# Storing the expert results of a mixture-of-experts layer through GpSimd with an index for each half row

## The reference

```python
g_idx = top_k(softmax(t @ rg_w + rg_b), 1)          # one of 4 groups
e_val, e_idx = top_k(softmax(e_logits of group), 2)  # two of its 8 experts
act = silu(t @ w_gate[e]) * (t @ w_up[e])            # 2048 -> 512
out = sum over the token's two experts of comb * (act @ w_down[e])   # 512 -> 2048
x = LN2(alpha * x + gate2 * out)
```

## Time and profile before

| | |
|---|---|
| median of three runs | 1796.48 us (1789.88 to 4247.93) |
| the profiled execution | 1792.82 us, span of the core 1791.0 us |
| TensorE's granted clock, mean | 0.968 |
| DMA, mean over the span | 332 GB/s, 593.75 MB |

### The profile page before, as it was taken

One profiled execution on the slowest core, in us unless ns is written; L12 is line 12 of the kernel. 1 busy time (PEld: TensorE's weight loads), 2 busy tenths in 40 slices (PEclk: granted clock), 3 DMA queues, 4 the chain that ended last, 5 costly groups with the idle time before them and its releaser, 6 DMA issues.

```text
span 1791.0 us, 23326 instructions
## 1 busy us (share of the span) xinstructions
PE 1676.3 (94%) x8973; PEld 723.8 (40%) x8974; DVE 487.6 (27%) x1288; ACT 286.0 (16%) x574; POOL 99.9 (6%) x168
## 2 busy tenths in 40 slices
PE   4999999999998998999999999999999999999994
PEld 2557555473443453333333333333333333333332
DVE  6556435130432554311111111110111111110115
ACT  3110000241223222111111111111111111111111
POOL 5001000410301000100000000000000000000010
PEclk9899999998899996999999999999999999999997
DMA  9996878941679315879989999999999999999963
GB/s 297 385 371 217 312 282 300 273 130 68 230 282 375 130 71 211 352 281 423 422 350 365 423 423 422 423 422 423 422 423 423 422 423 422 423 422 423 422 237 139
DMA packets 125446, 593.75 MB, mean 332 GB/s; under 512 B 13753, under 2 KB 18649, under 8 KB 66473
## 3 DMA queue, kind: packets, MB, share of 16 engines
q1 hardware_dynamic: 105984, 547.95, 76.6%
q0 software_dynamic: 9136, 24.54, 4.3%
q10 hardware_dynamic: 10274, 20.53, 3.2%
HBM read 565.78 MB, written 27.16 MB: 331 GB/s over the span
## 4 chain that ended last, share of the span: by engine, by line
PE 62%; DMA 33%; DVE 3%; ACT 1%; issue 1%; SPq 0%; POOL 0%; DVEq 0%; ACTq 0%; POOLq 0%
DMA ring<-in_exp_w_up 31%; PE bank L690 15%; PE bank L2251 6%; PE bank L707 5%; PE bank L2159 5%; PE bank L2008 4%; PE bank L665 3%; PE bank L333 3%; DMA ring<-in_ada_w 3%; PE bank L2202 2%; PE bank L2091 2%; PE bank L669 2%; PE bank L1986 2%; PE bank L678 1%; PE bank L755 1%; PE bank L1998 1%
## 5 line engine op out<-in xcount | busy, mean ns | idle before, releaser
L690 PE MATMUL bank<-ring,BC 128*64 128x512 f32 x2176 | 496.7, 595 | 32.9 <-DMA ring<-in_exp_w_up 32.0
L690 PEld LDWEIGHTS bank<-ring,BC 128*64 128x64 f32 x2176 | 178.7, 137 | 344.5 <-issue 268.9
L707 PE MATMUL bank<-ring,BC 128*64 128x512 f32 x1088 | 241.0, 595 | 0.0
L562 DVE TENSOR_TENSOR BC<-BC,bank 64x512 f32<-64x512 f32 x34 | 23.5, 692 | 501.0 <-ACT BC L625 501.0
L665 PE MATMUL bank<-H,BC 128*64 128x512 f32 x560 | 150.9, 599 | 1.7 <-DVE H L1871 1.7
L707 PEld LDWEIGHTS bank<-ring,BC 128*64 128x64 f32 x1088 | 75.1, 137 | 140.0 <-issue 135.9
L2251 PE MATMUL bank<-ring,MT 128*128 128x512 f32 x224 | 102.2, 610 | 1.0 <-issue 0.7
L2159 PE MATMUL bank<-ring,MT 128*128 128x512 f32 x192 | 85.4, 598 | 1.0 <-ACT X L1079 1.0
L625 ACT ACTIVATE BC<-bank 64x512 f32<-64x512 f32 x34 | 20.0, 589 | 394.4 <-PE bank L690 394.4
L665 PEld LDWEIGHTS bank<-H,BC 128*64 128x64 f32 x560 | 42.8, 136 | 90.8 <-issue 87.4
L669 PE MATMUL bank<-H,BC 32*64 32x512 f32 x280 | 75.2, 613 | 0.0
(11 more groups left out here) (528 smaller groups left out, 1499.5 us busy)
## 6 DMA issues: line engine op xcount, KB each, us to landing
ring<-in_exp_w_gate SPq DMA_DIRECT2D x128, 1024.0 KB, 21.5
ring<-in_exp_w_up SPq DMA_DIRECT2D x128, 1024.0 KB, 23.5
ring<-in_exp_w_down SPq DMA_DIRECT2D x128, 1024.0 KB, 20.7
ring<-in_ada_w SPq DMA_DIRECT2D x96, 1024.0 KB, 7.4
ring<-in_w_in SPq DMA_DIRECT2D x20, 1024.0 KB, 8.8
y_dram<-BC ACTq DMA_DIRECT2D x68, 256.0 KB, 7.8
ring<-in_w_out SPq DMA_DIRECT2D x16, 1024.0 KB, 10.2
y_dram<-X POOLq DMA_DIRECT2D x4, 1024.0 KB, 11.3
```

Of the source, the lines that this page charges most:

```text
L690: mm = pe.matmul(bank[64 * i:64 * i + 64, 2, :], xT[:, q // 2, k % 4, 64 * (q % 2):64 * (q % 2) + 64], ring[:, j, 512 * (k % 4):512 * (k % ...
L707: mm = pe.matmul(bank[64 * (c % 2):64 * (c % 2) + 64, 4 + c // 2, :], aT[:, j, :], ring[:, 8 + j, 512 * c:512 * c + 512], start=(j == 0), ...
```

## The change

GpSimd gets the same loop over the blocks and issues one indirect DMA for each block. It has 128 indices, one for each partition of YS: an index is a half row (4 KB) of `y_dram`, seen as 5120 half rows of 1024. The index of an empty slot is set beyond the bound, and the DMA has a bounds check that drops it without an error. VectorE works out the indices in each block with three small operations (`rows_of`) and a cast. The columns of a row are thus stored in the order q = 0, 2, 1, 3, and the tail reads them so (`y_cols`, `R_Q`). ScalarE issues no DMA in the loop.

The four early DMAs of zeros go. In their place GpSimd fills all of `y_dram` with 20 DMAs of 1 MB, from the constants in `con`, once the last weights before the experts have landed.

```diff
-    r[:, R_Q] = i // NS + 4 * SLOTS
+    r[:, R_Q] = i // NS % 2 * 2 + i // NS // 2 + 4 * SLOTS
+    r[:, R_W] = NO_ROW + 2 * (i % SLOTS) + i // SLOTS
...
+        def y_cols(q):
+            at = q % 2 * 2 + q // 2
+            return slice(512 * at, 512 * at + 512)
...
         def moe_pool(pool):
+            last = (len(plan) - 1) % PRE_RING
+            pool.wait_ge(landed[last], 16 * last_slot_uses[last])
+            for r in range(0, NBLK * SLOTS, P):
+                pool.dma_start(y_dram[r:r + P, :].rearrange("p (i n) -> p i n", i=4), spread_mid(con[:, 0:512], 4))\
+                    .then_inc(S("y_written"), 16)
...
+            def body(e):
+                pool.wait_ge(S("rint_ready"), since("rint_ready") + 3)
+                pool.wait_ge(S("y_row"), e)
+                pool.indirect_dma_start(y_dram.rearrange("r (c n) -> (r c) n", c=2),
+                                        bass.IndirectOffsetOnAxis(ap=y_row[:, :], axis=0),
+                                        YS[:, :, :].rearrange("p j n -> p (j n)"), None,
+                                        bounds_check=2 * NBLK * SLOTS - 1, oob_is_err=False)\
+                    .then_inc(S("y_written"), 16)
+            pool.wait_ge(S("rint_ready"), since("rint_ready") + 3)
+            expert_loops(pool, body, 1)
             tail_pool(pool)
...
+            def rows_of(e):
+                V.scalar_tensor_tensor(out=edge_past, in0=row_edge, scalar=row_at, in1=edge_sign,
+                                       op0=ALU.is_le, op1=ALU.mult, accum_out=row_valid).then_inc(S("row_valid"), 1)
+                dve.wait_ge(S("row_valid"), e + 1)
+                V.tensor_scalar(row_valid, row_valid, -float(NO_ROW), row_at, ALU.mult, ALU.add).then_inc(S("row_found"), 1)
+                dve.wait_ge(S("row_found"), e + 1)
+                V.tensor_scalar(row_at, row_at, 2.0 * SLOTS, None, ALU.add).then_inc(S("row_next"), 1)
+                dve.wait_ge(S("row_next"), e + 1)
...
                 select(e + 2)
+                dve.wait_ge(S("y_written"), Y_FILLED + 16 * e)
+                rows_of(e)
                 dve.wait_ge(used, len(plan) + (e + 1) * RING)
-                dve.wait_ge(S("y_written"), 32 * e + 32)
                 V.tensor_copy(YS[:, 1, :], bank[:, 5, :]).then_inc(S("ys_dve"), 1)
+                dve.wait_ge(S("ys_dve"), e + 2)
+                dve.wait_ge(S("ys_act"), e + 2)
+                V.tensor_copy(y_row[:, :], row_valid).then_inc(S("y_row"), 1)
...
+               V.tensor_scalar(row_edge[:, 0:E], first_of, 2.0 * SLOTS, float(NO_ROW), ALU.mult, ALU.add),
+               V.tensor_copy(row_at, rc[:, R_W:R_W + 1]),
+               V.memset(edge_sign[:, 0:E], 1.0), V.memset(edge_sign[:, E:], -1.0))
+            go(V.scalar_tensor_tensor(out=row_edge[:, E:], in0=count, scalar=2.0, in1=row_edge[:, 0:E],
+                                      op0=ALU.mult, op1=ALU.add))
...
-                act.wait_ge(S("y_written"), 32 * e + 32)
+                act.wait_ge(S("y_written"), Y_FILLED + 16 * e)
                 nc.scalar.copy(YS[:, 0, :], bank[:, 4, :]).then_inc(S("ys_act"), 1)
-                act.wait_ge(S("ys_act"), e + 2)
-                act.wait_ge(S("ys_dve"), e + 2)
-                for c in range(2):
-                    act.dma_start(y_dram[bass.ds(e * SLOTS, SLOTS), :].rearrange("s (j c n) -> c s j n", j=2, c=2)[c],
-                                  YS[64 * c:64 * c + 64, :, :]).then_inc(S("y_written"), 16)
...
-                for r in range(E * SLOTS, NBLK * SLOTS, P):
-                    n = min(P, NBLK * SLOTS - r)
-                    pool.dma_start(y_dram[r:r + n, :].rearrange("p (i n) -> p i n", i=4), spread_mid(zeros[0:n, :], 4))\
-                        .then_inc(S("spare_out"), 16)
...
-                act.wait_ge(S("spare_out"), 16 * -(-XB * SLOTS // P))
```

More of the change, by code:

```diff
@@ L44 @@
 BIG = 1e30
+NO_ROW = 65536
+Y_FILLED = 16 * NBLK * SLOTS // P
 NROW = 9
@@ L67 @@
 R_T = R_P + 1
-R_LTS = R_T + T // SLOTS + 1
+R_W = R_T + T // SLOTS + 1
+R_LTS = R_W + 1
 R_N = R_LTS + P
@@ L103, in constants @@
     r[:, R_P] = i
-    r[:, R_T:R_LTS] = [0] + [SLOTS * k + 1 for k in range(1, T // SLOTS + 1)]
+    r[:, R_W] = NO_ROW + 2 * (i % SLOTS) + i // SLOTS
+    r[:, R_T:R_W] = [0] + [SLOTS * k + 1 for k in range(1, T // SLOTS + 1)]
     m = np.zeros((P, M_N), np.float32)
@@ L228, in build @@
         slot_i = sb("slot_i", [P, 3, 2], I32)
+        y_row = sb("y_row", [P, 1], I32)
         sink = sb("sink", [P, NH])
@@ L493, in build, with expert_loops @@
         hi = slice(64, 128)
-        def expert_loops(eng, body):
-            with eng.Fori(0, E) as it:
+        row_edge = MODf[:, 1024:1024 + 2 * E]
+        edge_sign, edge_past = MODf[:, 1088:1088 + 2 * E], MODf[:, 1152:1152 + 2 * E]
+        row_at, row_valid = MODf[:, 1216:1217], MODf[:, 1217:1218]
+        def y_cols(q):
+            at = q % 2 * 2 + q // 2
+            return slice(512 * at, 512 * at + 512)
+        def expert_loops(eng, body, start=0):
+            with eng.Fori(start, start + E) as it:
                 body(it)
             extra = eng.value_load(rint[0:1, 0:1], min_val=0, max_val=XB)
-            with eng.Fori(E, NBLK) as it:
-                with eng.If(extra > it - E):
+            with eng.Fori(start + E, start + NBLK) as it:
+                with eng.If(extra > it - (start + E)):
                     body(it)
@@ L529, in moe_sp, with moe_dve @@
             tail_sp(sp)
-        def moe_dve(dve, rows_done, go, end_of, first_of, behind, lg, gm, m1, m2):
+        def moe_dve(dve, rows_done, go, count, end_of, first_of, behind, lg, gm, m1, m2):
             V = nc.vector
@@ L577, in moe_dve @@
                V.tensor_scalar(rsm[:, 6, 1:3, 0:2], slot_f[:, 0:2, :], float(SLOTS), None, ALU.add),
-               V.tensor_scalar(behind[0:1, 0:1], end_of[0:1, E - 1:E], float(E), None, ALU.subtract))
+               V.tensor_scalar(behind[0:1, 0:1], end_of[0:1, E - 1:E], float(E), None, ALU.subtract),
+               V.tensor_scalar(row_edge[:, 0:E], first_of, 2.0 * SLOTS, float(NO_ROW), ALU.mult, ALU.add),
[3 more added lines that the diff above has]
+                                      op0=ALU.mult, op1=ALU.add))
             V.tensor_reduce(xf[0:NBLK, 0:1].unsqueeze(2), after.unsqueeze(1), AX.X, ALU.add).then_inc(S("xf_ready"), 1)
@@ L630, in body @@
                 act.wait_ge(used, len(plan) + (e + 1) * RING)
-                act.wait_ge(S("y_written"), 32 * e + 32)
+                act.wait_ge(S("y_written"), Y_FILLED + 16 * e)
                 nc.scalar.copy(YS[:, 0, :], bank[:, 4, :]).then_inc(S("ys_act"), 1)
-                act.wait_ge(S("ys_act"), e + 2)
-                act.wait_ge(S("ys_dve"), e + 2)
-                for c in range(2):
-                    act.dma_start(y_dram[bass.ds(e * SLOTS, SLOTS), :].rearrange("s (j c n) -> c s j n", j=2, c=2)[c],
-                                  YS[64 * c:64 * c + 64, :, :]).then_inc(S("y_written"), 16)
             act.nop().then_inc(S("ys_act"), 1)
-            act.nop().then_inc(S("y_written"), 32)
             rows_out(0)
@@ L650, in moe_act @@
             extra = expert_loops(act, body)
-            act.wait_ge(S("y_written"), 32 * (extra + E) + 32)
+            act.wait_ge(S("y_written"), 16 * (extra + E) + Y_FILLED)
             act.nop().then_inc(S("y_all"), 1)
@@ L761, in tail_pe @@
                     for i in range(2):
-                        y = Y[:, b, i, 512 * q:512 * q + 512]
+                        y = Y[:, b, i, y_cols(q) if b < 2 else slice(0, 512)]
                         mm = pe.matmul(bank[:, at, :], DW[:, b, i, :], y, start=(i == 0), stop=(i == 1))
@@ L777, in tail_act @@
                     act.wait_ge(S("x_sum"), 2 + 4 * b + q)
-                    nc.scalar.activation(Y[:, b, 1, c], X[:, b, c], ACT.Square, accum_out=S2[:, b, 1, q:q + 1])\
+                    nc.scalar.activation(Y[:, b, 1, y_cols(q)], X[:, b, c], ACT.Square, accum_out=S2[:, b, 1, q:q + 1])\
                       .then_inc(S("x_sq"), 1)
@@ L800, in block @@
                     c = slice(512 * q, 512 * q + 512)
-                    add(Y_FROM[b] + q + 1, Y[:, b, 0, c], Y_BANKS[b][q], G2[:, c], X[:, b, c], S2[:, b, 0, q:q + 1])
+                    add(Y_FROM[b] + q + 1, Y[:, b, 0, y_cols(q)], Y_BANKS[b][q], G2[:, c], X[:, b, c], S2[:, b, 0, q:q + 1])
                 m = M2[:, b, :]
@@ L1957, in _ @@
                 xe, end_of, first_of, behind = (xt[:, i, :] for i in range(4))
-                go(V.tensor_tensor(xk, spread(count, 5), spread_mid(rc[:, R_T:R_LTS], E), ALU.is_ge))
+                go(V.tensor_tensor(xk, spread(count, 5), spread_mid(rc[:, R_T:R_W], E), ALU.is_ge))
                 go(V.tensor_reduce(xe.unsqueeze(2), xk, AX.X, ALU.add))
@@ L1967, in _ @@
                 go(V.tensor_reduce(slot_f[:, :, :].rearrange("p b i -> p i b").unsqueeze(3), both, AX.X, ALU.add))
-                moe_dve(dve, rows_done, go, end_of, first_of, behind, lg, gm, m1, m2)
```

(1 more changed line is left out.)

## The result

The changed kernel takes 1775.24 us (median of 6 runs, 1772.09 to 1779.38) against 1793.15 us before (median of 6, 1789.88 to 4247.93). The forecast was 1776 us. The profiled execution took 1774.79 us, with a span of 1773.0 us.

A forecast was written before the change was run, and what follows sets the result against it. TensorE was taken to bound early blocks and DMA bytes the late ones, from about 945 us on. 1792.8 us less 17 us for the stores, all other terms 0, gave 1776 us; range 1767 - 3 to 1790 us.

The forecast's parts named there:

- The bound: Expert loop: early blocks bound by TensorE at 28.37 us, late ones by DMA at 31.0 us; only late bytes count.
- The busiest engine sets the price: Late-loop stores: TensorE waits for the slowest engine's part; stores fall from 32.2 to 15.2 us, saving 17 us.
- four neighbouring partitions: Stores of blocks 7 to 32: each engine serves four neighbours, 91 to 99 half rows, 14.1 to 15.4 us; chance 0.50.
- Rivals 1 and 2: Loop stores: 1, even spread, 1767 us, chance 0.18; 2, eight neighbours or skipping saves nothing, 1785 to 1793 us, 0.24.
- The fill: Twenty DMAs in the idle stretch 600 to 662 us: takes 50 to 57 us, cost 0.
- the price of a slower fill: Before block 0: may end 22 us late before delaying block 0; beyond that, the excess costs microsecond for microsecond.
- VectorE: Three small operations and a cast per block, below 1 us in all, where VectorE idles: cost 0.
- The new wait: GpSimd's store waits for the cast, next copies for its landing: 51 us of cover against 3.1 to 16.6, cost 0.
- The tail: After the loop: ScalarE released 1 us earlier to 4 us later, under TensorE's 17.43 us; taken as 0, bounds 0 and +1.

The follow-up runs named there:

- Store nothing: The changed kernel with every index out of bounds, so no expert result is stored: 1761.75 us.
- store all: The changed kernel with the index of empty slots kept in bounds, so all 128 half rows are stored in each block: 1795.31 us.
- the layouts: The changed kernel with slots dealt out over groups of four partitions, 1771.24 us, or with slots 0 to 7 in partitions 0 to 3 and 32 to 35, 1788.80 us.
- the packed layout: The changed kernel with slots 0 to 7 in partitions 0 to 3 and 32 to 35: 1788.80 us, again 1788.46 us.
- Fill twice: The changed kernel with a scratch tensor of twice the rows, all filled by 40 DMAs: 1792.01 us.
- the fill at 150 us: The changed kernel with the twenty DMAs of the fill at 150 us, where the four of zeros stood: 1785.69 us.
- the dealt-out slots again: Second timing of the changed kernel with slots dealt out over the groups of four partitions: 1772.16 us.

## Why the prediction was right, step by step

**The bound.** Two regimes, and only the late one can gain: right. The early period did not move by more than 0.01 us. The late one began one to two blocks later, where I had two.

**The busiest engine sets the price.** I took four neighbouring partitions, 91 to 99 half rows, and 15.2 us for the stores of blocks 7 to 32, a saving of 17 us. The loop got 17.3 us shorter. "Store nothing" brings the loop down by another 1003.44 - 992.32 = 11.1 us, and "store all" puts 1019.10 - 1003.44 = 15.7 back, or 17.3 at an equal first block (28.42 against 30.09). So the skipped half rows are all of the gain.

The price of a half row was nearly right: I had 4096 B / 26.4 GB/s = 0.155 us. What I did not have is the packet of a dropped index. On the busiest engine a filled slot takes the place of a dropped one, so it adds only (30.46 - 29.90) / 4 = 0.14 us, and the dropped ones are in the base of 29.90, which I had as 29.8. The two pull against each other, and the late period came out at 30.45 where I had 30.4.

That the sum is so near is in part luck. Priced by the late periods, the saving is 26 x (31.02 - 29.90) for the full stores less 99 x 0.14 for the kept half rows, 15.3 us. The other 2 us lie at the ends of the regime: 1.1 up to block 15, and 0.9 in the last block, for which the kernel before waited on a load of 28.20 us where the others took 27.3. No run shows why, and nothing in the prediction foresaw them.

My reason for four neighbours was the share of today's stores, which is weak ground; the layouts tested it. At an equal first block 55, 99 and 160 half rows gave loops of 997.1 and 998.5, 1003.4, and 1014.5 and 1014.2 us. The Trainium skill, in "DMA: Bandwidth & Descriptors", section "The descriptor swizzle", states for a plain transfer to 128 partitions that an engine serves four partitions and the four that lie 32 further on. The periods behind 4 and 5 rows in the packed layout, 30.49 and 30.61 us, agree with it for a store by index.

**Rivals 1 and 2** would have given loops of 995 and 1013 us; both can nearly be had, but by choosing the layout. The chance of 0.18 for the even spread stood for a spread that the kernel doesn't have.

**The fill.** Cost 0: right, for the reason given. It took 58 us, just over my 50 to 57: from its first packet to its last it moved 363 GB/s, below the 371 that I had as the lower bound. In the price of a slower fill I was wrong twice: the place that it would stop is not block 0, from 684 us on, but the copies into YS, and the loop behind them from about 755 us on; and GpSimd does not keep forty such DMAs in flight.

**VectorE.** The added operations are in the timeline behind the selection, and the copy of bank 5 still comes after 3.94 us of idle time, where there were 5.25. They cost 0.28 + 0.08 + 0.21 + 0.15 us and 0.15 for the cast:

```profile
738.14 0.28 DVE L591 SCALAR_TENSOR_TENSOR MOD<-MOD 128x64 f32<-128x64 f32 x1
738.35 0.08 DVE L591 DVE_READ_ACCUMULATOR MOD<-MOD 128x1 f32 x1
738.47 0.21 DVE L594 TENSOR_SCALAR MOD<-MOD 128x1 f32<-128x1 f32 x1
738.72 0.15 DVE L596 TENSOR_SCALAR MOD<-MOD 128x1 f32<-128x1 f32 x1
742.81 0.69 DVE L609 COPY BC<-bank 128x512 f32<-128x512 f32 x1 [3.94 <-PE bank L748]
743.58 0.15 DVE L612 CAST y_row<-MOD 128x1 int32<-128x1 f32 x1
```

**The new wait.** The stores by index land in 7.7 us (median), as the plain ones did in 7.8. The 51 us of cover that I gave it are not there, though. "Fill twice" shows that a late copy stops ScalarE's silu of the next block, 14 us after the copy's turn, and not the down after it. The store is issued 1.5 us after its down and the next copy's turn comes 28.4 us after that down, so the cover is some 40 us. It was not needed.

**The tail.** Right: 57.0 us from the last down to the end before and after. ScalarE was released 0.8 us sooner, which TensorE's 17.43 us swallow:

```profile
1716.24 17.43 PE L796 MATMUL bank<-H,con 128*128 128x512 f32 x40 [0.30 <-issue]
1733.51 8.75 PE L804 MATMUL bank<-ring,MT 128*128 128x512 f32 x20
...
1721.12 1.28 ACT L695 ACT_TABLE_LOAD   x1 [4.46 <-DMA y_dram<-BC,y_row]
```

## What to carry to other kernels

Where a stage is bound by DMA, price a transfer by the bytes on its busiest engine and not by its mean: a store that skips rows saves only what the busiest engine skips, and a table of constants that deals the kept rows out gives the rest. Before pricing it, find from when on the DMA queue is never empty: a byte that leaves that stretch is time won, and a byte moved ahead of it is free only where the engines idle (the fill at 600 us was, the fill at 150 us was not). When bytes are moved into an idle stretch, look for what stands behind every wait on their landing, and for how many transfers the issuing queue takes at once.

## What the runs showed of the hardware that was not expected

- An index beyond the bound still makes a packet, one of 4 bytes: 4352 of them in 34 stores of 128 indices, some 10 ns each. The period with all indices dropped is 29.90 us where the weights alone account for 29.76.
- What a store by index costs goes by partitions: in a stage bound by DMA a filled slot on the fullest group of eight partitions (four, and the four 32 further on) adds 0.14 us to the period, up to eight of them, and one on another group adds nothing.
- GpSimd issued 31 DMAs of 1 MB (256 packets of 4 KB each) and then no other for 97 us, until the queue had nearly drained. With 20 nothing of the kind is seen. Whether the limit counts DMAs, packets or bytes is not shown.
- The time before the loop is not the same in all executions: block 0 starts at 710.6 to 717.3 us (the early fill aside) with nearly the same work ahead of it. The starts go with TensorE's clock, granted at one of its two levels (1.2 and 2.4 GHz): the mean over the first 712 us is 0.94 where block 0 starts at 712.5 us (the changed kernel, first row) and 0.93 where it starts at 716.5 us (the dealt-out slots again, second row). The other profiled executions go the same way: 0.94 with the starts up to 713.2 us, 0.93 with those from 715.6 us on. It blurs differences of 5 us between times that the loop shows sharply; how much of the scatter between the runs without a trace it makes is not shown.

```profile
0.00:712.00 712.00, 659.12 (x4407) 351.05 (x4408) 305.99 (x841) 141.98 (x346) 101.73 (x168) 0.94 0.76 271
```
```profile
0.00:712.00 712.00, 661.67 (x4393) 350.87 (x4394) 304.84 (x835) 140.91 (x344) 101.14 (x168) 0.93 0.76 271
```
